# Attention steps of a decoder layer: ScalarE's copy of the turned probabilities ahead of the exponential, gate work last in the step, a gate-free step behind each gate

## The reference

```
h = rms_norm(x, attn_norm)
(mq, mk, mv, nsq, kc, vc, ksl, vsl, kwn, vwn, ngate, mgate) = split(h @ w_in)
y_a = moba_attention(q_a, k_a, v_a)                 # 8 heads
y_b = nsa_attention(q_b, ...)                       # 8 heads, branches cmp, slc, win
g_a, g_b = split(sigmoid(mgate))
x = x + (g_a * (y_a @ w_br_moba) + g_b * (y_b @ w_br_nsa)) @ w_o
u = causal_dwconv(rms_norm(x, ffn_norm) @ w_up)
x = x + (gelu(u_act) * u_lin) @ w_down
x = x + sigmoid(x @ w_ple_gate) * (p @ w_ple)
```

## Time and profile before

| | |
|---|---|
| median of 3 runs | 969.73 us (968.89 to 970.35) |
| the profiled execution | 967.56 us, of which the span of the core is 965.8 |
| PE busy | 903.8 us (94%) |
| PE weight loads | 776.9 us (80%) |
| DVE, ACT, POOL busy | 439.6 (46%), 406.1 (42%), 407.6 (42%) us |
| mean granted TensorE clock | 0.974 |

### The profile page before, as it was taken

The page is one execution under the profiler, slowest core; times in us unless marked ns, Lnnn a source line. Parts: engine busy times, 40 slices in busy tenths (PEclk is TensorE's granted clock), DMA queues, the critical chain, the costliest instruction groups (busy, mean ns, idle before and its releaser), DMA issues.

```text
span 965.8 us, 13152 instructions
## 1 busy us (share of the span) xinstructions
PE 903.8 (94%) x4585; PEld 776.9 (80%) x4585; DVE 439.6 (46%) x969; ACT 406.1 (42%) x857; POOL 407.6 (42%) x413
## 2 busy tenths in 40 slices
PE   6898899896988878989999999999999999999998
PEld 6897898895968767877778788888888888888887
DVE  6717647756474654454541454443333343021034
ACT  5222554554553545464443455444444453232231
POOL 4632423423241424255646164445544445444450
PEclk8998999997999999999999999999999999999999
DMA  5755234135002112334653154333333333332313
GB/s 164 164 138 140 52 88 115 34 83 125 23 23 61 39 55 73 102 132 163 210 196 117 56 188 117 99 94 92 100 107 98 99 98 98 98 98 87 98 55 131
DMA packets 101363, 99.31 MB, mean 103 GB/s; under 512 B 15956, under 2 KB 76084, under 8 KB 101300
## 3 DMA queue, kind: packets, MB, share of 16 engines
q1 hardware_dynamic: 101247, 98.48, 34.9%
q10 hardware_dynamic: 53, 0.01, 0.0%
HBM read 87.58 MB, written 10.88 MB: 102 GB/s over the span
## 4 chain that ended last, share of the span: by engine, by line
PE 77%; DVE 13%; ACT 4%; issue 4%; DMA 1%; POOL 0%; SPq 0%; ACTq 0%; DVEq 0%; POOLq 0%
PE banks L1490 23%; PE banks L1492 23%; PE banks L1491 23%; DVE plain_arena L1266 2%; PE banks L1633 2%; DVE plain_arena L1238 2%; DVE split_arena L1154 1%; ACT split_arena L896 1%; PE banks L1544 1%; DVE split_arena L1301 1%; PE banks L1613 1%; ACT plain_arena L871 1%; PE banks L1612 1%; PE banks L1570 1%; DMA plain_arena<-in_x_dram 1%
## 5 line engine op out<-in xcount | busy, mean ns | idle before, releaser
L1490 PE MATMUL banks<-split_arena 128*128 128x512 f32 (+4 forms) x1228 | 468.7, 382 | 9.7 <-DVE split_arena L1170 6.1
L1491 PE MATMUL banks<-split_arena 128*128 128x512 f32 (+4 forms) x1228 | 457.7, 373 | 0.0
L1492 PE MATMUL banks<-split_arena 128*128 128x512 f32 (+4 forms) x1228 | 457.6, 373 | 0.0
L692 POOL TENSOR_TENSOR split_arena<-plain_arena,split_arena 128x512 fp32r<-128x512 f32 x184 | 241.1, 1323 | 256.4 <-ACT split_arena L912 237.1
L1490 PEld LDWEIGHTS banks<-split_arena 128*128 128x128 f32 x1228 | 234.2, 191 | 47.2 <-DVE split_arena L1170 6.4
L1492 PEld LDWEIGHTS banks<-split_arena 128*128 128x128 f32 x1228 | 233.9, 190 | 35.6
L1491 PEld LDWEIGHTS banks<-split_arena 128*128 128x128 f32 x1228 | 234.6, 191 | 32.1
L912 ACT ACTIVATE split_arena<-plain_arena 128x512 fp32r<-128x512 f32 x184 | 113.0, 627 | 192.8 <-PE banks L1492 180.7
L871 ACT ACTIVATE plain_arena<-plain_arena 128x128 f32<-128x128 f32 (+1 forms) x96 | 54.0, 563 | 146.1 <-DVE plain_arena L1266 145.9
L1448 DVE SCALAR_TENSOR_TENSOR plain_arena<-banks,plain_arena 128x511 f32<-128x511 f32 x44 | 32.7, 743 | 133.2 <-ACT plain_arena L1017 133.2
L707 POOL TENSOR_SCALAR plain_arena<-plain_arena 128x128 f32<-128x128 f32 (+1 forms) x64 | 41.7, 651 | 114.8 <-DVE plain_arena L1283 114.8
(11 more groups left out here) (161 smaller groups left out, 818.4 us busy)
## 6 DMA issues: line engine op xcount, KB each, us to landing
plain_arena<-in_w_up_dram SPq DMA_DIRECT2D x88, 256.0 KB, 3.2
plain_arena<-in_w_down_dram SPq DMA_DIRECT2D x44, 256.0 KB, 2.6
plain_arena<-in_w_in_dram SPq DMA_DIRECT2D x18, 512.0 KB, 4.6
plain_arena<-in_w_in_dram SPq DMA_DIRECT2D x32, 192.0 KB, 3.6
plain_arena<-in_x_dram SPq DMA_DIRECT2D x8, 512.0 KB, 5.0
gates<-plain_arena SPq DMA_DIRECT2D x16, 256.0 KB, 2.4
plain_arena<-skew SPq DMA_DIRECT2D x16, 256.0 KB, 3.6
plain_arena<-gates SPq DMA_DIRECT2D x16, 256.0 KB, 3.7
```

The source lines that it names most:

```text
L692: pool.tensor_tensor(W2l[:, c % RING, :], raw2[:, c % RING, :], W2h[:, c % RING, :].bitcast(F32), ALU.subtract).then_inc(w2_lo, 1)
L1490: nc.tensor.matmul(o, ah, bh, start=first, stop=False)
L1491: nc.tensor.matmul(o, ah, bl, start=False, stop=False)
L1492: return nc.tensor.matmul(o, al, bh, start=False, stop=last)
```

## The change

Three things. In the pairs 4 and 5 the gates' blocks take seven steps in place of eight, k = 1 to 7 and 9 to 15, the last with two blocks; steps k = 0, 8 and 16 have none. On ACT a step now runs `pt_high` and `exp` first, and `take_gate` with the copy into `Gh` behind them. On DVE `invert` and `pt_low` come right behind `bias`, then `rstd_end`, both halves of `normalise` and `gate_low`.

```diff
@@ GATE
         elif n < 6:
             for a in range(2):
-                for kt in range(KT):
-                    GATE[first_t[n] + 9 * a + kt] = (j, range(kt, kt + 1))
+                for b in range(7):
+                    GATE[first_t[n] + 8 * a + 1 + b] = (j, range(b, b + 1 if b < 6 else KT))
                 j += 1
@@ ACT, step t
                 for done in proj_end(t):
                     take_proj(*done)
                     squares_tile(*done)
+                if LAG <= t:
+                    pt_high(t - LAG)
+                if t < T:
+                    exp(t)
                 for j, end in gate_end.items():
                     if t == end + 1:
                         take_gate(j)
                         if j + 1 < NGATE:
                             act.wait_ge(graw_in, 16 * (j + 2))
                             nc.scalar.activation(Gh, graw, ACT.Copy).then_inc(g_hi, 1)
-                if t < T:
-                    exp(t)
-                if LAG <= t:
-                    pt_high(t - LAG)
                 if n in range(4, NPAIR) and k == 6:
                     gather_strip(n)
@@ DVE, step t
                 if t < T:
                     bias(t)
+                if 1 <= t <= T:
+                    invert(t - 1)
+                if t >= LAG:
+                    pt_low(t - LAG)
                 if t - 1 in NORM:
                     rstd_end()
-                if 1 <= t <= T:
-                    invert(t - 1)
-                if t - 1 in NORM:
                     normalise(NORM[t - 1], 0)
+                    normalise(NORM[t - 1], 1)
                 for j, end in gate_end.items():
                     if t == end + 1 and j + 1 < NGATE:
                         gate_low(j + 1)
-                if t >= LAG:
-                    pt_low(t - LAG)
@@ DVE, step t, behind w_low and rstd_begin
-                    if t - 1 in NORM:
-                        normalise(NORM[t - 1], 1)
```

## The result

The changed kernel takes 956.32 us (954.36 to 957.88, 4 runs) against 969.31 us (968.73 to 970.35, 4 runs) for the kernel before, run beside it: a ratio of 0.9875, 95% interval 0.9854 to 0.9895, so 13.0 us less. The direction was right, the size was not. One execution of the kernel before, beside the first four experiments, took 3131.91 us; no ratio counts it.

The account below looks back on a forecast made before the run. PE was taken to bound the kernel, busy 94% of the span, its idle and half clock the prize. Gains of 14.6 less costs of 9.8 gave 4.8 us less, 964.9 from the median 969.73; own range 962 to 967.5.

Parts of the forecast that it names:

- 49, wait and clock: Step 49: the gate-free step removes PE's 2.5 us wait for the new gate's weights, and 1.7 us of half clock.
- 66, wait and clock: Step 66: the free step shortens PE's wait from 3.56 to 1.0 us; gain 2.5, plus 1.7 of clock.
- 76: Steps 76 to 78: `pt_low` starts 1.5 us earlier, idle falls to 0.5, the low stretch goes; 3.2 us gained.
- 60 to 64: Last normalisation: `invert` ahead of `rstd_end`, POOL's `scale` starts 1.2 us earlier; 1.3 us gained, bounds 0.7 and 4.1.
- 4: Gate taken over at step 4: gate work behind exp makes `vec_high` later; 1.3 us lost, PE having no idle there.
- 12 and 20, wait and clock: Gates taken at steps 12 and 20: 1.4 us later each, PE's idle 2.7, new low stretches costing 3.4 together.
- 40 to 47: Steps 40 to 46: `w_low`, behind both halves of `normalise`, comes 1.5 us later; 0.3 lost, bounds -1.5 and 1.5.
- 82: Gate taken at step 82, where no free step stands: its weights come later, a new PE wait of 1.5 us.
- Part 2: `pt_high` and `pt_low` ahead: gains of 3.2 at steps 76 to 78, 1.3 at 93, 0.4 at 70 and 87, 1.3 at 60 to 64.
- A: Rival, the clock is kinder: no low stretch at steps 12 and 20; 8.2 us less, 961.5; chance 0.17.
- B: Rival, the clock gives nothing back: remaining idles keep half clock as often as today; no change, 970; chance 0.16.
- C: Rival, slower: DVE waits in `gate_low` for the later copy at 13 steps, 19.5 us in all; 974.6; chance 0.12.

Follow-up runs that it names:

- e3: The kernel before with only ScalarE's new order, DVE's order and the gates' steps as before: 976.26 us, ratio 1.0095.
- e11: The kernel before with `pt_high` first on ScalarE, then gate work, then exp, DVE's order untouched: 960.71 us, ratio 0.9914.
- e1: The kernel before with only the gate-free step, both engines' orders as before: 958.52 us, ratio 0.9906.
- e8: The kernel before with only `pt_high` first on ScalarE and `pt_low` ahead of `gate_low` on DVE: 954.93 us, ratio 0.9862.
- e5: The changed kernel with the gate's take-over and copy ahead of exp again on ScalarE, `pt_high` still first: 946.53 us, ratio 0.978.
- e2: The kernel before with both new orders (ScalarE and DVE), the gates' steps as before: 964.77 us, ratio 0.9968.
- e9: The kernel before with the free step, `pt_high` and `pt_low` ahead, gate work ahead of exp, `invert` directly behind `bias`: 945.17 us, ratio 0.9754.

## Why the forecast missed

Each term against the stretches of the table, after minus before, with 0.7 us added or taken off for each gate block that moved over the edge of a stretch (0.7 is what the stretch 52 to 59, without any wait of its own, grew by for its one block more):

| place | forecast | measured |
|---|---|---|
| 49, wait and clock | -4.2 | -3.7 |
| 66, wait and clock | -4.2 | -4.2 |
| 76 | -3.2 | -2.8 |
| 93 | -1.3 | -1.1 |
| 70 and 87 | -0.4 | -1.5 |
| 60 to 64 | -1.3 | -2.1 |
| 8 and 16 | none | -0.8 |
| 4 | +1.3 | +1.6 |
| 12 and 20, wait and clock | +6.2 | +1.2 |
| 28 | +0.5 | 0.0 |
| 40 to 47 | +0.3 | +1.0 |
| 82 | +1.5 | +1.6 |
| sum | -4.8 | -10.8 |

- **The step that failed** is that at 12 and 20 "PE's idle becomes 1.28 + 1.4 = 2.7 us", with "both as new low stretches", 6.2 us in all. The places took 1.2: the idle became 1.46, with the clock at full. That is 5.0 of the 6.0 us that the steps were off by; e3, with ScalarE's order alone, took 3.9 there.
- I had added ScalarE's 1.4 us to the idle of the old orders and put at nothing there what else the change does. That is two things. First, with `pt_high` ahead of the exponential DVE waits for it 0.47 us in place of 1.18; that half alone (e11) takes 2.1 us out of these two places. It is also why bias(11) starts 1.5 us earlier (145.24, 146.75 before) and bias(12) 1.3: bias(11) stands 2.2 us behind its scores in e11 and after, 3.3 before. Second, DVE's order: against e3 the change saves 2.6 us at the two places, with hardly less idle (2.7 and 2.9 us for 2.9 twice) but in two parts and without the low stretches.
- Behind exp(12) `gate_low` waits for its copy and starts 0.7 us later (153.61, 152.91 before), and `vec_low` still starts at 154.33 in place of 154.32, since `pt_low`, which stood between the two, has already run. Behind its own scores it is 0.5 later. Which move of DVE's order does the most, only the traces suggest, and that the low stretch stays away because the idle is parted fits them but is not shown: the kernels differ in more than that.
- The clock was also read too short: the forecast speaks of four stretches of half clock in the attention steps, and the trace of before has seven, 30.7 us. The three that it left out, at 114.1, 226.7 (10.2 us long) and 271.1, have two of the three that grew. And of PE's idle before 450 us 14 us lie ahead of the steps, so that "nearly all of it in the attention steps" was too much.
- **The gains** at 49, 66, 76 and 93 held to within 0.5 each, that at 76 with luck: its idle fell by 1.2 us and not 1.5, and the 1.7 of the clock comes without the new orders too (e1). The waits held as well: the free step at 49, the idle left at 66 (0.93 for 1.0) and the new one at 83. That last one in the trace, answering to the earlier trace rows:

```profile
385.79 0.42 ACT L868 ACTIVATE plain_arena<-plain_arena 128x256 f32<-128x256 f32 x1 [0.70 <-DVE plain_arena L1276]
386.59 1.05 ACT L975 ACTIVATE split_arena<-plain_arena 128x1024 fp32r<-128x1024 f32 x1
388.42 0.50 PE L1488 MATMUL banks<-split_arena 128*128 128x512 f32 x1 [1.35 <-DVE split_arena L1170]
```

- 1.35 us of idle where 1.5 was forecast. Seen by itself the pair of `pt_high` and `pt_low` was under-sized: the forecast gave Part 2 6.2 us, with `invert` in it, and e8 gives 13.2 without. I had looked mostly at places where PE waits for `pt_low`; `pt_high` also stood in front of `vec_high`, and DVE waited for it.
- **60 to 64** was 2.1 for 1.3. Steps 60 to 62 of DVE, POOL and PE, answering to the earlier trace rows:

```profile
329.28 0.16 DVE L1283 RECIPROCAL plain_arena<-plain_arena 128x1 f32<-128x1 f32 x1
330.05 0.60 DVE L1118 SCALAR_TENSOR_TENSOR plain_arena<-plain_arena 128x16 f32<-128x16 f32 x1
331.52 2.50 DVE L1238 TENSOR_TENSOR plain_arena<-plain_arena 128x512 f32<-128x512 f32 x4
329.97 0.66 POOL L707 TENSOR_SCALAR plain_arena<-plain_arena 128x384 f32<-128x384 f32 x1
330.69 0.55 PE L1631 MATMUL banks<-plain_arena 128*128 128x128 f32 x3 [0.77 <-POOL plain_arena L707]
332.97 0.63 PE L1542 MATMUL banks<-plain_arena 128*128 128x128 f32 x4 [1.73 <-DVE plain_arena L1238]
```

- `scale` on POOL takes 0.66 us in place of 1.60, as forecast, and PE's idle of 2.41 falls to 0.77. The rule of the Trainium skill that was weighed here (GPSIMD Engine Reference, Specifications) is borne out too: beside it, L1118 of `rstd_end` takes 0.60, where the same instruction takes 0.17 at 331.11 with POOL idle. But that is 0.4 us, not the whole gain.
- **The losses** elsewhere: 4 and 82 were right to 0.3, but 4 by luck. The forecast put gate work behind the exponential there; what grew is the wait for `normalise`, from 2.05 us to 3.40, and it is as long in e5, without that gate work, and 2.07 in e3, with it and the old DVE order. At 40 to 47 the cost was 1.0 for 0.3, inside its bounds of 1.5: the first vector turn there waits 2.84 us for `normalise`, and half clock lasts 3.4 us longer.

```profile
271.66 0.63 PE L1542 MATMUL banks<-plain_arena 128*128 128x128 f32 x4 [2.84 <-DVE plain_arena L1238]
```

- **The rivals.** A had the right place, no new low stretch at 12 and 20, and its 961.5 was the nearest. It missed that the idle itself would hardly grow. B fell by the time, though half clock adds up to the same 30.7 us: full clock came back behind 49, 66 and 76 and was lost at other places. Its sentence from the Trainium skill (TensorE: Matmul & The Clock Gate, A second HAM failure mode) has weak support: near 62 no idle is over 1.73, two of them (0.77 and 1.73) lie within 3 us, and a low stretch of 6.8 us follows. But e2 has the same two idles there, 0.76 and 1.73, at full clock. C fell as a sum, but DVE does stand in front of `gate_low` for the later copy, 1.60 us at step 12 and 1.52 at 65; e5, which ends that along with the later `vec_high`, takes 9.8 us out, half of C's 19.5.
- **What was to show it**: no wait at 49, one of 0.93 at 66, one of 1.35 at 83, L1301 under 4, and the three low stretches gone, all as said. L1249 up with 2.7 at 13 and 21 did not come. And the sign of being wrong did: `vec_low` at 12 is not later, and the losses were too large.
- **Open.** The medians differ by 13.0 us and the steps by 10.8; I count 1.7 ahead of step 0 as chance, and 0.5 I can't place. What decides whether half clock comes behind an idle is open as well, and with it how much of any single place is chance.

## What to carry to other kernels

In an engine that runs its instructions in order, sort them by when their inputs are ready, and put filler work, such as the gates' here, into the idle ahead of the instruction that is waited for, not behind it: that alone was 9.8 us. When two engines' orders change together, price them together, step by step; alone they cost 8 and 19 us here, and as a pair they gained 3. Before a low-clock stretch is put down to a change, look for it in another execution of the same code; and count it by how busy PE is in it.

## What the runs showed of the hardware

- In the attention steps of the thirteen traces PE has 76 idles of 1.9 us and more. Behind or around 65 of them the granted clock is 0.50 for 3.4 us or longer; behind 11 it stays full, among them 3.37 in e5 at step 4 and 3.02 in e9 at 62. The same idle at the same place comes out either way: 2.05 at step 4 with half clock before, 2.07 without it in e1; 1.98 at 78 with it before, 1.99 without it in e1; 1.73 at 62 with it after, without it in e2. So in this kernel the length of an idle does not settle it.
- 3.4 us more at half clock cost 1.6 us near step 78, where PE had work for all of it, and 1.1 near step 30, where it stood still for some of it (before against e1, one execution each).
- DVE instructions of 128x16 elements take 0.16 to 0.18 us when no POOL instruction runs (all 120 of them before and after), and up to 1.26 while one does, half of them 0.6 and more. POOL's scaling of 128x384 elements takes 1.52 to 1.60 us beside DVE's 128x512 multiplications (5 times before) and 0.58 to 0.67 otherwise (43 times).
